# All four quarters of the second feed-forward product by seven block products, in a new order and with paired VectorE instructions

## The reference, cut to what matters

```python
hn = rmsnorm(h, norm2_g[l])
h = h + jnp.square(jax.nn.relu(hn @ w_ff1[l])) @ w_ff2[l]   # w_ff1 1024x4096, w_ff2 4096x1024
return rmsnorm(h, final_g)
```

## Time and profile before

| | us |
|---|---|
| median of 3 runs | 1193.88 |
| lowest, highest | 1193.0, 1194.52 |
| the profiled execution's own time | 1193.29 |
| its span, first to last instruction | 1191.5 |
| PE busy | 1147.7 (96%) |
| DVE busy | 756.9 (64%) |
| POOL busy | 515.0 (43%) |
| ACT busy | 409.1 (34%) |

### The profile page before, as it was taken

The page is one execution under the profiler, slowest core; times in us unless marked ns, Lnnn a source line. Parts: engine busy times, 40 slices in busy tenths (PEclk is TensorE's granted clock), DMA queues, the critical chain, the costliest instruction groups (busy, mean ns, idle before and its releaser), DMA issues.

```text
span 1191.5 us, 18120 instructions
## 1 busy us (share of the span) xinstructions
PE 1147.7 (96%) x6722; PEld 929.0 (78%) x6722; DVE 756.9 (64%) x1376; ACT 409.1 (34%) x783; POOL 515.0 (43%) x517
## 2 busy tenths in 40 slices
PE   7999999999999999999999999999999999999997
PEld 6777777777887887877776777777888888888886
DVE  3888564787823576564886777762358767667563
ACT  3125111134732332211225544420324544443434
POOL 4885344354536587655833433466551000000032
PEclk9999999999999999999999999999999999999999
DMA  7222111115013222224441111123525647565422
GB/s 249 80 92 65 55 53 52 39 54 142 2 35 98 72 88 89 86 73 106 175 136 53 38 53 54 54 71 90 229 89 127 164 156 171 143 169 114 89 71 89
DMA packets 32765, 115.09 MB, mean 97 GB/s; under 512 B 3633, under 2 KB 6065, under 8 KB 31921
## 3 DMA queue, kind: packets, MB, share of 16 engines
q1 hardware_dynamic: 27040, 93.47, 25.0%
q0 software_dynamic: 3264, 12.58, 5.6%
q10 hardware_dynamic: 2384, 7.99, 2.2%
HBM read 107.74 MB, written 2.10 MB: 92 GB/s over the span
## 4 chain that ended last, share of the span: by engine, by line
PE 80%; DVE 10%; ACT 3%; POOL 3%; issue 2%; DMA 1%; SPq 0%; DVEq 0%; POOLq 0%; ACTq 0%
PE acc L299 19%; PE acc L300 17%; PE acc L301 17%; PE aux L301 3%; PE aux L300 3%; PE aux L299 3%; PE aux L2089 3%; POOL w_lo L1977 2%; PE aux L825 2%; PE aux L815 2%; PE aux L2070 1%; PE aux L366 1%; DMA residual<-x 1%; PE acc L519 1%; PE aux L806 1%
## 5 line engine op out<-in xcount | busy, mean ns | idle before, releaser
L1977 POOL TENSOR_TENSOR w_lo<-w_raw,w_hi 128x256 fp32r<-128x256 f32 x352 | 296.2, 872 | 7.1
L1969 POOL CAST w_hi<-w_raw 128x1024 fp32r<-128x1024 f32 x108 | 118.9, 1101 | 380.3 <-issue 272.2
L299 PE MATMUL acc<-ht_hi,w_hi 128*128 128x512 f32 x672 | 271.5, 404 | 6.4 <-POOL w_lo L1977 2.3
L301 PE MATMUL acc<-ht_hi,w_lo 128*128 128x512 f32 x672 | 263.2, 392 | 0.0
L300 PE MATMUL acc<-ht_lo,w_hi 128*128 128x512 f32 x672 | 263.0, 391 | 0.0
L299 PEld LDWEIGHTS acc<-ht_hi,w_hi 128*128 128x128 f32 x672 | 126.8, 189 | 37.0 <-POOL w_lo L1977 6.1
L301 PEld LDWEIGHTS acc<-ht_hi,w_lo 128*128 128x128 f32 x672 | 126.7, 189 | 27.3
L300 PEld LDWEIGHTS acc<-ht_lo,w_hi 128*128 128x128 f32 x672 | 127.1, 189 | 24.3 <-issue 1.0
L299 PE MATMUL acc<-w_hi,ht_hi 128*128 128x512 f32 x256 | 105.4, 412 | 0.1
L2028 POOL DMA_DIRECT2D ff_block<-units x12 | 14.7, 1336 | 205.4 <-DVE ff_w_lo L1745 205.4
L301 PE MATMUL acc<-w_hi,ht_lo 128*128 128x512 f32 x256 | 100.1, 391 | 0.0
(11 more groups left out here) (477 smaller groups left out, 2159.1 us busy)
## 6 DMA issues: line engine op xcount, KB each, us to landing
w_raw<-units SPq DMA_DIRECT2D x140, 512.0 KB, 3.6
ff_block<-units SPq DMA_DIRECT2D x12, 1024.0 KB, 8.9
ff_block<-units POOLq DMA_DIRECT2D x12, 1024.0 KB, 12.1
cmp_w<-w_kv ACTq DMA_DIRECT2D x4, 1024.0 KB, 7.0
residual<-x SPq DMA_DIRECT2D x4, 512.0 KB, 7.0
k_turned<-k_split SPq DMA_DIRECT2D x8, 256.0 KB, 3.7
result<-final_rows SPq DMA_DIRECT2D x4, 512.0 KB, 2.6
consts_sb<-consts SPq DMA_DIRECT2D x1, 1120.5 KB, 7.8
```

Source lines behind the costliest of these rows:

```text
L299: nc.tensor.matmul(bank, ah, bh, start=start, stop=False)
L301: return nc.tensor.matmul(bank, al, bh, start=False, stop=stop)
L1969: nc.gpsimd.tensor_copy(w_hi[:, slot], raw[:, j]).then_inc(hi_split, 1)
L1977: done = nc.gpsimd.tensor_tensor(w_lo[:, slot, kk, cols], raw[:, j, kk, cols], w_hi[:, slot, kk, cols].bitcast(F32), ALU.subtract)
```

## The change

- Quarter 3 of the second product also goes by seven products (numbers 21 to 27); the plain product, its units, `ff_hi`, `ff_lo` and POOL's `ff_low` and `end_low` are gone. There are no more units to interleave with, so products 21 to 27 follow one another on PE.
- The products of a quarter come in another order. Product 0 now uses a block sum (B12 + B22) and an operand sum (`s3`, by `low_k_sum`). POOL adds B22 to B12 (`two_blocks`) ahead of each quarter; for quarter 0 this stands before POOL's splits of the first eight feed-forward units, and waits for the load of B12. SP loads B12 first.
- In products 22 to 27 `p_hi`, `p_lo` alternate between two buffers (`end_buffer`; the second lies where `w_hi`, `w_lo` were).
- `product_low` works on two k-tiles at once (128x1024 instead of 128x512), `product_out` on both banks of a product at once (`aux_pair`), so 10 instructions of 128x1024 a quarter.
- At the end, C12 and C21 take `common` beside the last products; the last product runs row tile by row tile (12 matmuls each) and feeds rows 2 and 3; the halves that the final norm treats as old and new differ by row.

The diff, cut to its core:

```diff
-            weight_slab(pe, U_LAST, ff_hi, ff_lo, SLAB_LAST, True, operand=(on["fflo_s"], 1))
-            slab, unit, paired = SLAB_END - 1, U_LAST + UPS, UPS - 2
-            for j in range(paired):
-                for b in range(4):
-                    weight_piece(pe, unit + j, j, b, 2 * j, ff_hi, ff_lo, slab, j == 0, False, True)
-            for b in range(4):
-                if b == 0:
-                    pe.wait_ge(w_split, N_LOADS)
-                rows = slice(b * P, (b + 1) * P)
-                for k in range(TILES):
-                    done = split_product(pe, acc[b][:], (ff_hi[:, 2 * paired + k, rows], ff_lo[:, 2 * paired + k, rows]),
-                                         (p_hi[:, k], p_lo[:, k]), False, k == TILES - 1)
-                done.then_inc(unit_used if b == 3 else acc_ready[b], 2 if b == 3 else 1)
-
-
+            for i in range(PRODUCTS):
+                product_on_tensor(pe, QUARTERS - 1, i)
...
+        B11, B12, B21, B22 = range(4)
         BLOCK_AT = {B11: (0, 0), B12: (0, 1), B22: (1, 1), B21: (1, 0)}
+        FIRST_END = PRODUCTS * (QUARTERS - 1) + 1
 
         def block_buffer(q, of):
-            if of in (B11, B21):
-                return of if q % 2 == 0 else B11 + B21 - of
-            return of
+            return of if of == B11 else 1 + (of - 1 + q) % 3
 
         def product_block(q, i):
-            return block_buffer(q, (B11, B21, B11, B12, B11, B22, B11)[i])
+            return block_buffer(q, (B12, B11, B21, B12, B11, B22, B12)[i])
+
+        def end_buffer(n):
+            return int(n >= FIRST_END and (n - FIRST_END) % 2 == 0)
...
+            if n < N_PRODUCTS - 1:
+                for k in range(TILES):
+                    if k % 2 == 0:
+                        pe.wait_ge(p_split, P_SPLIT + 2 * n + k // 2 + 1)
+                    part(k, 0)
+                    part(k, 1).then_inc(prod_used, 1)
+            else:
+                pe.wait_ge(p_split, P_SPLIT + 2 * n + 2)
                 for tt in range(2):
-                    cols = slice(tt * P, (tt + 1) * P)
-                    done = split_product(pe, aux[2 * (n % 2) + tt][:],
-                                         (a_hi[:, n % 2, k, cols], a_lo[:, n % 2, k, cols]),
-                                         (p_hi[:, k], p_lo[:, k]), k == 0, k == TILES - 1)
-                done.then_inc(prod_used, 1)
+                    for k in range(TILES):
+                        done = part(k, tt)
+                    done.then_inc(prod_used, 1)
...
-            if i in (2, 4, 6):
-                act.wait_ge(chain_sum, 16 * (3 * q + i // 2))
-            elif i == 3:
-                act.wait_ge(pair_sum, 16 * (q + 1))
+            if i in (0, 4):
+                act.wait_ge(pair_sum, 16 * (2 * q + 1 + i // 4))
+            elif i in (3, 6):
+                act.wait_ge(chain_sum, 16 * (2 * q + i // 3))
             else:
                 act.wait_ge(block_in[product_block(q, i)], BLOCK_IN + 16 * (q + 1))
             for k in range(TILES):
-                if n:
-                    act.wait_ge(prod_used, PROD_USED + TILES * (n - 1) + k + 1)
-                nc.scalar.activation(p_hi[:, k], blk[product_block(q, i)][:, k], ACT.Copy).then_inc(p_high, 1)
+                if n == FIRST_END:
+                    if k % 2 == 0:
+                        act.wait_ge(unit_used, N_LOADS - 1 + k // 2)
+                elif n:
+                    act.wait_ge(prod_used, PROD_USED + TILES * (n - (1 if n < FIRST_END else 2)) + k + 1)
+                nc.scalar.activation(p_hi[end_buffer(n)][:, k], blk[product_block(q, i)][:, k], ACT.Copy).then_inc(p_high, 1)
...
-            def product_low(n, k):
+            def product_low(n, part):
                 q, i = divmod(n, PRODUCTS)
-                eng.wait_ge(p_high, P_HIGH + TILES * n + k + 1)
-                V.tensor_tensor(p_lo[:, k], blk[product_block(q, i)][:, k], p_hi[:, k].bitcast(F32),
-                                ALU.subtract).then_inc(p_split, 1)
+                eng.wait_ge(p_high, P_HIGH + TILES * n + 2 * part + 2)
+                k = slice(2 * part, 2 * part + 2)
+                V.tensor_tensor(p_lo[end_buffer(n)][:, k], blk[product_block(q, i)][:, k],
+                                p_hi[end_buffer(n)][:, k].bitcast(F32), ALU.subtract).then_inc(p_split, 1)
...
+                homes = (((C22, ALU.subtract), (C21, ALU.add)),
+                         ((common[:], ALU.add), (C11, ALU.add)),
+                         ((C11, ALU.add),),
+                         ((common[:], ALU.subtract),),
+                         ((C22, ALU.subtract), (C12, ALU.subtract)),
+                         ((C12, ALU.subtract),))[i] if i < 6 else ((C21, ALU.add),)
+                for at, (home, op) in enumerate(homes):
+                    if n == 1 and at == 0:
+                        done = V.tensor_copy(home, bank)
+                    else:
+                        done = V.tensor_tensor(home, home, bank, op)
...
+            def low_k_sum(q):
+                if q:
+                    eng.wait_ge(a_split, A_SPLIT + PRODUCTS * (q - 1) + 6)
+                eng.wait_ge(on["ff_squared"], KD * q + TILES)
+                V.tensor_tensor(s3[:], ff[q % 2][:, LOW_K, EARLY_T], ff[q % 2][:, LOW_K, LATE_T],
+                                ALU.subtract).then_inc(a_sum, 1)
+
+            def late_sums(q):
+                eng.wait_ge(on["ff_squared"], KD * (q + 1))
+                V.tensor_tensor(s1[:], ff[q % 2][:, HIGH_K, LATE_T], ff[q % 2][:, LOW_K, LATE_T],
+                                ALU.subtract).then_inc(a_sum, 1)
+                eng.wait_ge(a_sum, A_SUM + 4 * q + 2)
+                V.tensor_tensor(s2[:], s1[:], ff[q % 2][:, LOW_K, EARLY_T], ALU.add).then_inc(a_sum, 1)
+
+            def last_sum(q):
+                eng.wait_ge(a_split, A_SPLIT + PRODUCTS * q + 1)
+                eng.wait_ge(a_sum, A_SUM + 4 * q + 3)
+                V.tensor_tensor(s3[:], s2[:], ff[q % 2][:, HIGH_K, EARLY_T], ALU.subtract).then_inc(a_sum, 1)
...
-            for k in range(TILES):
-                product_low(0, k)
+            low_k_sum(0)
+            product_low(0, 0)
+            product_low(0, 1)
             operand_low(0)
             unit_low(U_FF + 2 * UPS)
...
+            q, first = QUARTERS - 1, PRODUCTS * (QUARTERS - 1)
+            product_low(first + 1, 0)
+            product_low(first + 1, 1)
+            operand_low(first + 1)
+            late_sums(q)
+            product_out(first)
+            product_low(first + 2, 0)
+            product_low(first + 2, 1)
+            operand_low(first + 2)
+            last_sum(q)
+            for i in (2, 3):
+                product_out(first + i - 1)
+                product_low(first + i + 1, 0)
+                product_low(first + i + 1, 1)
+                operand_low(first + i + 1)
+            product_out(first + 3)
+            product_low(first + 5, 0)
+            product_low(first + 5, 1)
+            operand_low(first + 5)
+            eng.wait_ge(prod_out, PROD_OUT + first + 4)
+            step(V.tensor_tensor(C22, C22, common[:], ALU.subtract))
+            product_out(first + 4)
+            product_low(first + 6, 0)
+            product_low(first + 6, 1)
+            operand_low(first + 6)
+            eng.wait_ge(prod_out, PROD_OUT + first + 5)
+            V.tensor_tensor(C12, C12, common[:], ALU.subtract)
+            step(V.tensor_tensor(C21, C21, common[:], ALU.add))
+            product_out(first + 5)
...
+            def add_last(t):
+                eng.wait_ge(prod_used, PROD_USED + TILES * (N_PRODUCTS - 1) + t - 1)
+                V.tensor_tensor(X[:, t, early_half], X[:, t, early_half], aux_pair[(N_PRODUCTS - 1) % 2][:, t - 2],
+                                ALU.add).then_inc(on["last_added"], 1)
...
+            scaled(0)
+            scaled(1)
+            add_last(2)
+            add_last(3)
+            scaled(2)
+            scaled(3)
...
-            for at in (B11, B12, B22, B21):
+            for at in (B12, B11, B21, B22):
...
-                                          (U_B2 + RING, U_O2, 4), (U_O2, U_FF + 2 * UPS, 1)):
+                                          (U_B2 + RING, U_O2, 4), (U_O2, U_FF, 1)):
...
+            def two_blocks(q):
+                if q:
+                    pool.wait_ge(pair_sum, 16 * 2 * q)
+                pool.wait_ge(block_in[block_buffer(q, B12)], BLOCK_IN + 16 * (q + 1))
+                add_block(q, block_buffer(q, B12), B22, pair_sum)
+
+            two_blocks(0)
+            with pool.Fori(U_FF // RING, (U_FF + 2 * UPS) // RING) as i:
+                for j in range(RING):
+                    split(i * RING + j, i, j, True, 1)
+            for q in range(QUARTERS):
+                pool.wait_ge(p_split, P_SPLIT + 2 * (PRODUCTS * q + 1))
+                add_block(q, block_buffer(q, B12), B11, chain_sum)
+                pool.wait_ge(p_split, P_SPLIT + 2 * (PRODUCTS * q + 2))
+                add_block(q, B11, B12, pair_sum)
```

(4 more changed lines are left out.)

249 lines of the change are left out of this document (81 added, 168 removed).

## The result

The changed kernel takes 1206.41 us in the median (1203.97 to 1208.82, 4 runs); the kernel before, in the same session, 1193.44 (1192.73 to 1194.52, 4 runs). The ratio is 1.0108, 95% interval 1.0085 to 1.0130: slower by 1.1%. That is inside the range given, by 0.1 us at its upper end, and two of the four runs (1207.0 and 1208.82) lie above it. The profiled execution took 1205.83 us (span 1204.0) against 1193.29 (1191.5): 12.5 us more, where the sum of the prediction had 9.9.

What follows compares the result with a forecast made beforehand. TensorE, busy for 96% of the span, was taken to set the pace, with VectorE holding it in the last quarter. 4.4 + 1.5 + 4.0 = +9.9 us on 1193.3 gave 1203.2 us, range 1199.5 to 1206.5.

Steps and rivals of the forecast that it cites:

- The saving, -5.4: Quarter 3 has 168 matmuls in place of 192 on TensorE: -5.4 us if nothing else is late.
- Start, +4.4 for POOL's wait: Before the first feed-forward unit, TensorE stands while POOL waits for a block, issues its adding DMA and splits: +4.4 us.
- the clock's fall: Rival, 18%: behind the idle time at the start the clock halves, costing 1.5 to 3 us more, 1205.4 in total.
- Relu, +1.5: Before the first interleaved unit, VectorE's relu comes later and TensorE waits for its bank: +1.5 us.
- Quarters 0 to 2, nothing: In quarters 0 to 2 VectorE's extra work and the adding DMAs cost nothing, as TensorE's unit covers them.
- Last quarter: Products 21 to 27: VectorE cannot keep up, TensorE stands 5.8 us, so the saving is lost; +4.0 us in all.
- The rival of cheap pairs: Rival, 5%: 128x1024 VectorE instructions over pairs cost some 0.6 us, not 1.14, so VectorE never holds TensorE: 1194.2.
- The tail: After the last matmul, VectorE's remaining work ends the last scaling at T+51.2 against T+47.2: +4.0 us.
- The adding DMA for product 24: Rival, 10%: in the last quarter the DMA adding B11 lands too late for product 24: +1.5 us, 1204.7.
- a free wait at POOL: Rival, 6%: POOL's wait for the block at the start costs nothing, giving 1198.8.

Runs made afterwards that it cites:

- less_vector: relu_first without six VectorE instructions of the last quarter (three second targets, three corrections by common), leaving out part of the output; 1193.11 us, ratio 0.9992.
- add_later: The changed kernel with POOL's splits of the first four feed-forward units put before the block wait and adding DMA; 1199.76 us, ratio 1.0050.
- keep_warm: The changed kernel with 18 extra matmuls, result unused, in TensorE's idle time before the first feed-forward unit; 1205.09 us, ratio 1.0089.
- wait_only: add_later with POOL's wait for the block back before the split, the adding DMA still behind it; 1203.61 us, ratio 1.0089.
- relu_first: add_later with VectorE's relu before the operand's low part, and ScalarE making the unit's high part before the operand's; 1198.46 us, ratio 1.0038.
- extra_quarters: relu_again with eighteen extra VectorE instructions, result unused, spread over quarters 0 to 2; 1198.44 us, ratio 1.0033.
- relu_again: relu_first unaltered, run once more as a base in a later session; 1198.42 us, ratio 1.0033 to the kernel before.
- changed_again: The changed kernel unaltered, run again in a second session on another chip; 1206.41 us, ratio 1.0101 to the kernel before.
- one_buffer: relu_first with one pair of weight buffers for the block's parts to the end in place of two; 1219.50 us, ratio 1.0217.

## Why the prediction was right, and where its sum fell short

- **The saving, -5.4.** Right that 24 matmuls go (6722 to 6698), and that none of it arrives. TensorE ended at T + 44.0 against T + 43.9 before. less_vector, whose output is incomplete, shows that VectorE is what keeps it back: with six of its instructions less TensorE ends at T + 40.7, and the stretch is 45.7, 1.5 under the 47.2 from before, though the tail is still longer.
- **Start, +4.4 for POOL's wait.** Measured 4.64. The mechanism was right, and the size came out in part by luck, since errors cancelled. (The prediction's own rows give 4.2 to 4.4 and not 4.6 as the upper end: 849.1 + 1.4 + 3.52 = 854.0.) The block took 5.9 to land, 5.8 in the earlier trace rows; the adding DMA held POOL for 1.0 before the CAST, less than the 1.2 to 1.4 forecast, but the CAST took 1.46 beside it where the earlier trace rows has 1.04. The Trainium skill's fit ("DMA: Bandwidth & Descriptors", Anatomy of one DMA) is for DMAs that GpSimd issues, and this load is SP's, with three more behind it. The 3.0 that it would have given for this term, an estimate, is not what was seen: the trace's own duration was the one to use.
- **The step that failed.** This term was priced as idle time alone, at a clock held at 1.00, and the clock's fall was kept as a rival at 18%. It fell in both profiled executions of the changed kernel, and 1.67 us at 1.2 GHz came on top; add_later took both away (6.65), keep_warm the second alone (1.3 to 1.6). The rival's price, 1.5 to 3, held, and its total of 1205.4 is nearer to the median than the 1203.2 given. Without it the sum is short, and the median is inside the range only because the range was drawn to cover this rival. The row that it rested on the earlier trace rows gives 4.3 us from the last matmul's end (1184.7 to 1189.0), not 4.1, and the stand computed was 4.2 to 4.6: at the same size, 18% was too little. Nor do the runs show an edge at that length: behind the 3.0 of wait_only the clock held, and behind gaps of 2.5 in the last quarter it fell in several kernels. The Trainium skill ("TensorE: Matmul & The Clock Gate", HAM oscillation) says that idle gaps of this order bring half rate. The trace agrees at the start, 0.66 in the window behind the stand.
- **Relu, +1.5.** Measured 1.6, and 1.3 came back with relu_first.
- **Quarters 0 to 2, nothing.** Right, 244.93 against 244.82, and extra_quarters shows how much room there was: more than 20 us of VectorE.
- **Last quarter.** The waits forecast were 0.8, 2.6, 1.4 and 0.9 before products 22, 23, 24 and 27, and the profile has 0.7, 2.5, 1.2 and 0.9. The pitch of 1.14 over bank pairs, which no row of before showed, was 1.135. (The rival of cheap pairs put its turning point at 0.9; 31 instructions fit into 32.6 us from 1.05 down.) 27 was to start at T + 38.4: it did (1187.96 - 1149.54). The tail was forecast at T + 51.2 and is T + 50.9, so +3.7 for +4.0.
- **The adding DMA for product 24** was in time; the wait before it ended with VectorE's low part. That rival (10%), and those of a free wait at POOL and of cheap pairs, fell.
- **Outside the sum** lie 0.8 us of the profiled pair that were lost before the change begins: 1.6 to the clock at 100 to 140 us, 0.8 made good around it.

## What to carry to other kernels

Before counting matmuls saved, count the queue that feeds them: here a block product costs TensorE 5.44 us and VectorE five or six instructions of 1.14, which is free as long as a unit of the first product lies between and is the bound as soon as it does not. A new wait on an engine that splits weights should be costed with the instruction that it is for, and with what stands behind it in that engine's queue; putting the next units' work first gave back 6.65 us for the move of one loop. And TensorE's idle time of 4.6 us had two prices here, itself and the matmuls behind it at half clock.

## What was not expected of the hardware

- The clock also falls behind shorter gaps, and not in every run. In the last quarter of relu_again, relu_first and add_later it fell at product 23's wait of 2.5 us, or within 1.4 us behind it, where changed_again and wait_only, with the same wait, and the changed kernel kept 1.00 in their profiled executions. Windows of relu_again:

```profile
1150.00:1155.00 5.00, 3.71 (x17) 2.74 (x15) 5.00 (x6) 2.52 (x5) 0.00 (x0) 1.00 1.06 208
1155.00:1160.00 5.00, 3.96 (x11) 3.16 (x12) 5.00 (x5) 1.25 (x2) 0.00 (x0) 0.66 0.41 82
```

- There it cost next to nothing: the stretch is 51.0 to 51.2 in those kernels and 50.9 to 51.0 in the three others. VectorE sets the pace, and TensorE at half rate only uses up waits that it would have had (the wait before product 24 is gone from the list). At the start, where TensorE is the pace, the same fall cost 1.67.
- In one_buffer, where every product has a gap of 3.3 us before it, the clock was 0.84 to 0.92 in the windows of the stretch, and from the second of its gaps on some 1.5 us a period went to it beside the gap itself. What decides between a fall and none after a given gap, these runs don't settle.
- The kernel before alone scatters by 3.9 us over 22 runs on one chip (1192.71 to 1196.59), and its mean clock goes with it: 0.998 in the fastest, 0.994 in the slowest. In the profiled executions of the kernels here, dips lie in parts that no kernel touched (100 to 140 us in eight of fourteen, 380 to 400 us in all but one_buffer), so a difference of 1 us is better read from the stretch in the profile than from medians.
